# State-space stage of a two-block model: the loads, the convolution's filter taps and its gates in another order

## The reference, cut to what matters

```python
xbc = silu(dw_conv_centred(xbc, conv_w, conv_b))          # 5 taps along the tokens, per channel
xs, bm, cm = split(xbc)                                   # x per head, B and C per group
dt = softplus(dt + dt_bias)
# per direction, chunk by chunk, h carried on:
cum = cumsum(dt_c * -exp(a_log))
h_new = h * exp(cum[-1]) + einsum(b_c, exp(cum[-1:] - cum), x_c * dt_c)
seg = exp(where(lower, cum[i] - cum[j], -inf))
y = einsum(c_c . b_c, seg, x_c * dt_c) + einsum(c_c, h) * exp(cum)
# after both directions:
y = (y + d * x) * silu(z)
```

## Time and profile before

| | us |
|---|---|
| median of 3 runs | 5115.91 |
| lowest and highest | 5101.51, 5119.13 |
| the profiled execution | 5113.0 |
| its span | 5111.2 |
| start of the stage to the first step of group 0 | 72.70 |
| group 0, 1, 2, 3 | 96.90, 92.20, 92.20, 69.80 |

### The profile page before, as it was taken

One profiled execution on the slowest core, in us unless ns is written; L12 is line 12 of the kernel. 1 busy time (PEld: TensorE's weight loads), 2 busy tenths in 40 slices (PEclk: granted clock), 3 DMA queues, 4 the chain that ended last, 5 costly groups with the idle time before them and its releaser, 6 DMA issues. The chain is left out here.

```text
span 5111.2 us, 87975 instructions
## 1 busy us (share of the span) xinstructions
PE 4426.0 (87%) x38358; PEld 3445.9 (67%) x38358; DVE 2546.7 (50%) x3657; ACT 1593.3 (31%) x2530; POOL 502.2 (10%) x464
## 2 busy tenths in 40 slices
PE   7999969999897678786998777779999898887999
PEld 5888848877777456563332364568888786676787
DVE  4556667767775665542111315644442312675553
ACT  3222223333332453431000314432222212663332
POOL 0000021111110456000000003300000000000000
PEclk9999989999998789897999888889999999898999
DMA  6656720000001020426999520021122134112232
GB/s 244 228 201 217 268 76 23 15 15 14 14 6 38 19 70 17 170 79 250 421 421 422 212 95 18 24 103 58 62 67 71 66 115 143 38 62 87 83 103 91
DMA packets 165710, 604.18 MB, mean 118 GB/s; under 512 B 24192, under 2 KB 37376, under 8 KB 139984
## 3 DMA queue, kind: packets, MB, share of 16 engines
q1 hardware_dynamic: 152096, 538.78, 29.3%
q0 software_dynamic: 13232, 59.77, 3.0%
HBM read 527.03 MB, written 71.46 MB: 117 GB/s over the span
## 5 line engine op out<-in xcount | busy, mean ns | idle before, releaser
L2010 PE MATMUL f_acc<-f_a_lo,f_w_hi 128*128 128x512 f32 x4048 | 1034.9, 358 | 64.4 <-DVE f_a_lo L2232 30.5
L2010 PEld LDWEIGHTS f_acc<-f_a_lo,f_w_hi 128*128 128x128 f32 x4048 | 666.4, 190 | 187.2 <-issue 42.0
L2010 PE MATMUL f_acc<-f_a_lo,f_w_lo 128*128 128x512 f32 x2288 | 687.0, 356 | 0.0
L1999 DVE TENSOR_TENSOR f_w_lo<-f_w_raw,f_w_hi 128x1024 fp32r<-128x1024 f32 (+1 forms) x176 | 228.4, 1298 | 539.2 <-ACT f_w_hi L1994 539.2
L2010 PEld LDWEIGHTS f_acc<-f_a_lo,f_w_lo 128*128 128x128 f32 x2288 | 380.3, 190 | 67.7
L1994 ACT CAST f_w_hi<-f_w_raw 128x1024 fp32r<-128x1024 f32 (+1 forms) x176 | 194.8, 1107 | 611.0 <-DMA f_w_raw<-in_ffn_w_up 219.5
L2010 PE MATMUL i_acc<-i_x_hi,i_w_hi 128*128 128x512 f32 (+1 forms) x1024 | 306.6, 355 | 15.0 <-DVE i_x_lo L2787 10.0
L390 DVE COPY_PREDICATED rw_work<-rw_mask_x,rw_big 128x512 f32<-128x512 uint8 x288 | 238.4, 880 | 153.0 <-PE rw_big L690 147.9
L2010 PE MATMUL i_acc<-i_x_lo,i_w_hi 128*128 128x512 f32 (+1 forms) x1024 | 305.4, 354 | 0.0
L2010 PE MATMUL i_acc<-i_x_hi,i_w_lo 128*128 128x512 f32 (+1 forms) x1024 | 305.1, 353 | 0.0
L1417 PE MATMUL ex_big<-ex_w,ex_xe 128*64 128x512 f32 x1024 | 233.4, 611 | 31.8 <-DMA ex_w<-in_exp_w 31.1
(11 more groups left out here) (521 smaller groups left out, 8089.0 us busy)
## 6 DMA issues: line engine op xcount, KB each, us to landing
ex_w<-in_exp_w SPq DMA_DIRECT2D x192, 1024.0 KB, 16.3
i_mod_rows<-in_ada_rows SPq DMA_DIRECT2D x128, 512.0 KB, 4.7
f_w_raw<-in_ffn_w_up SPq DMA_DIRECT2D x88, 512.0 KB, 3.5
i_w_raw<-in_w_in_both SPq DMA_DIRECT2D x44, 512.0 KB, 3.6
f_w_raw<-in_ffn_w_down SPq DMA_DIRECT2D x32, 704.0 KB, 4.0
i_w_raw<-in_w_in_lat SPq DMA_DIRECT2D x40, 512.0 KB, 4.7
pt<-i_stage POOLq DMA_DIRECT2D x22, 768.0 KB, 5.9
f_w_raw<-in_hgrn_w_both SPq DMA_DIRECT2D x24, 512.0 KB, 3.5
```

Of the source, the lines that this page charges most:

```text
L1999: dve.tensor_tensor(self.view(self.w_lo, u), self.view(self.w_raw, u), self.view(self.w_hi, u).bitcast(F32), ALU.subtract).then_inc(self.r ...
L2010: op = pe.matmul(acc[:, a:b], part[:, k], xs[:, k0 + k, a:b], start=(first and k == 0 and part is w_hi and xs is x_hi), stop=(last and k = ...
```

## The change

It touches the start and the loop, on SP, DVE and ACT. PE's and POOL's instructions stand in the same order as before; PE's wait for the constants counts five transfers instead of seven.

- SP issues the step-size rows, their bias and the filter parameters (a semaphore `par_in` of their own), then group 0's rows, and behind these the five other constants.
- DVE clears only the three pads of each row of `raw` that no transfer or copy writes.
- At the start ACT permutes pair 0 ahead of the step-size chain, pairs 1 and 2 inside it; DVE takes taps of pairs 0, 1 and 2 between the chain's instructions and `silu` of pairs 0 and 1 ahead of the last product on `kinds`; ACT's gate of pair 2 stands behind `turned(0, 0..5)`.
- In the loop pair 1's taps stand at s = 4 (two), 5 and 6, pair 2's at s = 7 (two), 8 and 9; the gates of pairs 0 and 1 at s = 7 and their `silu` at s = 7 and 8; the gate of pair 2 at s = 10, its `silu` at s = 11.

```diff
+        TAPS = {4: ((1, 1), (1, 2)), 5: ((1, 3),), 6: ((1, 4),), 7: ((2, 1), (2, 2)), 8: ((2, 3),), 9: ((2, 4),)}
...
                 sp.dma_start(dtf[:, 0, :], pt[DT_T, 0:64, :]).then_inc(S["dt_in"], 16)
-                for dst, src in ((bias[:], dt_bias), (alog[:], a_log), (ident[:], consts["ident"]), (tri[:], consts["tri"]), (ones[:], consts["ones"]),
-                                 (skip[:], d_skip), (par[:].rearrange("p (g t) n -> p g t n", g=NG), params.rearrange("g p t n -> p g t n"))):
-                    sp.dma_start(dst, src).then_inc(S["const_in"], 16)
+                sp.dma_start(bias[:], dt_bias).then_inc(S["dt_in"], 16)
+                sp.dma_start(par[:].rearrange("p (g t) n -> p g t n", g=NG), params.rearrange("g p t n -> p g t n")).then_inc(S["par_in"], 16)
                 sp.wait_ge(S["pads"], 1)
                 load_group(0)
+                for dst, src in ((alog[:], a_log), (tri[:], consts["tri"]), (ident[:], consts["ident"]), (ones[:], consts["ones"]), (skip[:], d_skip)):
+                    sp.dma_start(dst, src).then_inc(S["const_in"], 16)
...
-                dve.memset(raw[:], 0.0)
+                dve.memset(raw[:, :, 0:2], 0.0)
+                dve.memset(raw[:, :, LAT + 2:LAT + 4], 0.0)
+                dve.memset(raw[:, :, CV_W - 2:CV_W], 0.0)
...
                 dve.drain().then_inc(S["dt_ready"], 1)
+                for k in range(1, CONV):
+                    conv_tap(0, 0, k)
+                dve.wait_ge(S["dt_abs"], 1)
...
+                conv_tap(0, 1, 1)
+                conv_tap(0, 1, 2)
+                dve.wait_ge(S["dtt_copied"], 1)
...
+                conv_tap(0, 1, 3)
+                conv_tap(0, 1, 4)
+                dve.wait_ge(S["const_in"], 80)
                 dve.tensor_copy(ident_r[:], ident[:])
...
                 dve.drain().then_inc(S["cums_done"], 1)
+                conv_tap(0, 2, 1)
+                conv_tap(0, 2, 2)
+                silu(0, 0)
+                silu(0, 1)
                 dve.wait_ge(S["kinds_done"], 1)
                 dve.tensor_tensor(flat(WJ), flat(WJ), flat(DT), ALU.mult)
                 dve.drain().then_inc(S["kinds_done"], 1)
-                for pair in range(3):
-                    for k in range(1, CONV):
-                        conv_tap(0, pair, k)
-                for pair in range(3):
-                    dve.drain()
-                    silu(0, pair)
+                conv_tap(0, 2, 3)
+                conv_tap(0, 2, 4)
+                dve.drain()
+                silu(0, 2)
...
-                            if 4 <= s < 8:
-                                conv_tap(g + 1, 1, s - 3)
-                            if s >= 8:
-                                conv_tap(g + 1, 2, s - 7)
-                            if s in (8, 9):
-                                silu(g + 1, s - 8)
-                    if more:
-                        dve.drain()
-                        silu(g + 1, 2)
+                            for pair, k in TAPS.get(s, ()):
+                                conv_tap(g + 1, pair, k)
+                            if s in (7, 8):
+                                silu(g + 1, s - 7)
+                            if s == 11:
+                                silu(g + 1, 2)
...
+                act.wait_ge(S["par_in"], 16)
+                permute(0, 0)
                 act.wait_ge(S["dt_ready"], 1)
...
+                act.wait_ge(S["const_in"], 80)
                 act.activation(alog[:], alog[:], ACT.Exp)
                 act.drain().then_inc(S["dt_abs"], 1)
+                permute(0, 1)
...
-                for pair in range(3):
-                    gate(0, pair)
-                for k in range(TURNS):
+                gate(0, 0)
+                gate(0, 1)
+                for k in range(6):
+                    turned(0, k)
+                gate(0, 2)
+                for k in range(6, TURNS):
                     turned(0, k)
...
-                        if more and s == 8:
+                        if more and s == 7:
                             gate(g + 1, 0)
                             gate(g + 1, 1)
+                        if more and s == 10:
+                            gate(g + 1, 2)
...
-                    if more:
-                        gate(g + 1, 2)
```

More of the change, by code:

```diff
@@ L847, in ssm @@
         TURNS = 9
-        names = ("const_in dt_in dt_ready dt_abs dtt_ready dtt_copied dta_ready cum_ready cums_done kinds_done masks_done pads group_in permuted tap_done conv_done "
+        TAPS = {4: ((1, 1), (1, 2)), 5: ((1, 3),), 6: ((1, 4),), 7: ((2, 1), (2, 2)), 8: ((2, 3),), 9: ((2, 4),)}
+        names = ("const_in dt_in par_in dt_ready dt_abs dtt_ready dtt_copied dta_ready cum_ready cums_done kinds_done masks_done pads group_in permuted tap_done conv_done "
                  "sig_done silu_done tr_ready tr_copied xw_done state_ready h_done inter_ready tmp_done row_ready exp_done g_done xdt_done xs_done skip_done "
@@ L923, in silu @@
                     dve.tensor_tensor(tiles(g, pair), tiles(g, pair), ex_tiles(pair), ALU.mult).then_inc(S["silu_done"], 1)
-                dve.memset(raw[:], 0.0)
+                dve.memset(raw[:, :, 0:2], 0.0)
+                dve.memset(raw[:, :, LAT + 2:LAT + 4], 0.0)
+                dve.memset(raw[:, :, CV_W - 2:CV_W], 0.0)
                 dve.memset(one[:], 1.0)
                 dve.drain().then_inc(S["pads"], 1)
-                dve.wait_ge(S["const_in"], 112)
-                dve.wait_ge(S["dt_in"], 16)
+                dve.wait_ge(S["dt_in"], 32)
                 dve.tensor_scalar(dtf[:, 1, 0:LAT].rearrange("p (c r) -> p c r", r=ROWS), dtf[:, 0, 0:LAT].rearrange("p (r c) -> p c r", c=GRID), bias[:, 0:1], None, ALU.add)
@@ L932, in _ @@
                 dve.drain().then_inc(S["dt_ready"], 1)
+                for k in range(1, CONV):
+                    conv_tap(0, 0, k)
+                dve.wait_ge(S["dt_abs"], 1)
+                dve.scalar_tensor_tensor(dtf[:, 0, :], dtf[:, 1, :], 0.0, dtf[:, 2, :], ALU.max, ALU.add)
+                dve.drain().then_inc(S["dtt_ready"], 1)
+                conv_tap(0, 1, 1)
+                conv_tap(0, 1, 2)
+                dve.wait_ge(S["dtt_copied"], 1)
+                for c in range(6):
+                    dve.scalar_tensor_tensor(kinds[:, DTA, c].rearrange("p d h -> p (d h)"), alog[:], -1.0, kinds[:, DT, c].rearrange("p d h -> p (d h)"), ALU.mult, ALU.mult)
+                dve.drain().then_inc(S["dta_ready"], 1)
+                conv_tap(0, 1, 3)
+                conv_tap(0, 1, 4)
+                dve.wait_ge(S["const_in"], 80)
                 dve.tensor_copy(ident_r[:], ident[:])
@@ L936, in _ @@
                 dve.drain().then_inc(S["masks_done"], 1)
[L937 to L943, removed]
                 dve.wait_ge(S["cum_ready"], 1)
@@ L1050, in _ @@
                 act.drain().then_inc(S["dtt_copied"], 1)
-                for pair in range(3):
-                    permute(0, pair)
+                permute(0, 2)
                 act.wait_ge(S["cum_ready"], 1)
@@ L1164, in cum_rows @@
                     last.then_inc(S["row_ready"], 1)
-                pe.wait_ge(S["const_in"], 112)
+                pe.wait_ge(S["const_in"], 80)
                 pe.wait_ge(S["dtt_ready"], 1)
```

## The result

The changed kernel takes 5129.7 us (median of 10 runs), the one before 5118.2 (10 runs): a ratio of 1.0031, 95% interval 1.0017 to 1.0044. The loss is real and small, some 11 to 20 us.

What follows compares the result with a forecast made beforehand. PE was taken to be held by waits: at the start, for exponentials behind a gate awaiting DVE's tap, and for pair 2's silu. 5.0 us a group, 15.0 for three, less 2.5: +12.5, 5128 us, range 5100 to 5145.

Steps and rivals of the forecast that it cites:

- start: Before group 0: rows and first turn come earlier, turn 6 waits for pair 2's gate; 2.5 us gained, bounds 0 to 5.9.
- (a): Loop step 4: two added DVE taps make PE wait for `tmp` in step 5; 0.6 us cost, bounds 0 to 1.4.
- (b): Loop step 7: PE's wait behind pair 1's gate moves up from step 8 and grows 2.9 us, to 6.0.
- (c): Loop step 10: pair 2's gate ahead of the exponentials, behind a late tap; 4.4 us cost, bounds 1.2 to 7.3.
- (d): Group's end: the gate and ACT's idle time go; 2.9 us gained, bounds 2.9 and 5.65.
- POOL's instructions alternate: Upper bound for step 4's added taps: POOL's instructions alternate with all of DVE's taps; 1.4 us cost.
- the waits vanish: Rival: loop taps run free and gates find columns done; 20.5 us less, 5095, lowest 5084; chance 0.08.
- Only an exchange: Rival: step 7's wait equals step 8's old one, pair 2's gate costs what the end returns; 5113 to 5122; chance 0.20.
- Slower by more: Rival: both loop waits leave PE slow for long; 29 us more, 5143; chance 0.20.
- The longer switch: Rival: each of six added table changes holds ACT another 1.28 us; 7.7 us more, 5136; chance 0.02.
- Table time: Theory of the experiments: gate and two table loads (1.28 + 1.49 + 1.28 us) cost that wherever they stand in the loop.
- Crowded DVE: Theory of the experiments: the doubled taps make `tmp` and the state late in the loop; the gates matter little.

Runs made afterwards that it cites:

- change_again: The changed kernel, unaltered, profiled and measured once more: 5136.6 us, ratio 1.0048 to the kernel before.
- start_only: The new start of the change with the loop of the kernel before: 5105.6 us.
- fewer_taps_at_4: The changed kernel without the two taps of step 4, which are left out of the convolution: 5116.1 us.
- gates_at_8: The changed kernel with the gates of pairs 0 and 1 back at s = 8, their silu at s = 8 and 9, taps still doubled: 5122.0 us.
- no_switch: The changed kernel with Exp in place of Sigmoid in the gates of groups 1 to 3, so no table loads beside them: 5124.9 us.
- no_last_tap: The changed kernel without the tap of step 9, left out of the convolution; gate and loads of step 10 stay: 5117.4 us.

## Why the prediction was right

It gave 5128 us (+12.5); measured are +11.5 and +19.6. That the first comparison comes within 2 us of the forecast is partly luck. The forecast added 5.0 us for a group, and the groups grew by 8.0 on average in the first profile and by 5.9 in change_again; in the first profile the rest of the program happened to be 8.0 us shorter than in the profile before (4749.2 against 4757.2). The second median, 5136.6, lies above the 5124 to 5134 to which the forecast was narrowed. The mechanism, though, is the one that was forecast: both waits, for late taps behind which the exponentials stand, and a small gain at the start and at the groups' ends. Its terms against the two profiles of the change, each as a difference from the same steps of before:

| | predicted | first profile, groups 0, 1, 2 | change_again |
|---|---|---|---|
| start | -2.5 | -2.8 | -2.9 |
| (a) + (b), steps 3 to 8 | +3.5 | +2.4, +3.8, +3.5 | +2.8, +2.7, +2.8 |
| (c), step 10 | +4.4 | +6.2, +6.2, +6.1 | +4.6, +4.6, +4.6 |
| (d), end | -2.9 | -1.9, -3.7, -1.7 | -3.0, -3.0, -3.0 |
| steps 0 to 2 | 0 | 0.0, +0.9, 0.0 | 0.0, +2.4, +2.4 |
| step 9 | 0 | 0.0, +2.2, 0.0 | 0.0, 0.0, 0.0 |

**The start** held step by step: rows at 1652.01 (1652.2 predicted), table load 1683.57 (1684.5), turn 0 at 1690.37 (1691.7), turn 6 at 1705.02 (1705.8), 0.2 to 1.3 us early, of which 0.55 is that this execution reached the stage sooner. start_only shows this gain by itself.

**(a)** 0.6 was the right kind and no fixed size: PE waits 0.95 us for `tmp` in step 5 in group 2 and nothing in two groups of change_again, but 3.12 in group 1 of the first profile, over twice the upper bound of 1.4. Four taps in a row took 7.11 in group 2 with POOL busy beside them, where the start before has sixteen in 16.16.

The bound "POOL's instructions alternate" has a rule for it in the Trainium skill ("SBUF — State Buffer", SBUF: two separate sides): DVE and GpSimd share a port pair, and where a DVE instruction has two inputs in SBUF and GpSimd's reads SBUF, the one that starts first holds the pair for its whole instruction and blocks the other. The rows agree in that a tap took 1.78 against 1.01; that each waited for whole instructions of the other, they do not show.

**(b)** was right in its cause in five of the six groups: the wait is moved a step up and lengthened by the taps put ahead. Its sum was right because two sizes were wrong in opposite directions. PE waits 4.3 to 4.6 and not 6.0, since pair 1's last tap ran nearly undisturbed (1.95 where 3.2 was reckoned); but the slow work behind the wait is 2.9 in group 2 (13.81 less 6.60 and 4.34) and up to 3.5 in change_again, and not 1.87. In group 1 of the first profile the +3.8 is a coincidence of sums: the wait for the gate was 1.44 there, and the rest is DVE's late `tmp`. fewer_taps_at_4 takes the lengthening away and leaves the wait; gates_at_8 takes the wait away; no_switch takes 1 to 2.5 us off the step of 13.8 to 14.6.

**(c)** stands too: PE got its product 12.1 us behind the state product of step 9, predicted 12.3 (1882.5 less 1870.2). That the slow work behind that wait would cancel against the waits that step 10 has anyway held in change_again and not in the first profile: after 4.05 and 4.04 us of waiting, the granted clock was 0.66 for the next 5.1 us in the one and 0.51 for 6.6 in the other. The lines of change_again:

```profile
1884.91 1.66 PE L1232 MATMUL ss_big<-ss_xdt,ss_seg 128*128 128x64 f32 x8 [4.05 <-POOL ss_seg L1144]
...
1884.91:1890.00 5.09, 5.09 (x30) 4.99 (x31) 0.00 (x0) 0.61 (x2) 2.27 (x2) 0.66 0.54 187
```

That goes with the difference of some 1.6 us a group, by which (c) was sized too small in the first profile. no_last_tap shows that all of (c) hangs on the late tap.

**(d)** came out at 3.0 in change_again. In the first profile groups 0 and 2 gave back less; PE was still at the low clock ahead of the end there (turn 6 took 1.91 in group 2 and 1.14 in group 1, which gave back 3.7).

**Not in the sum:** that ACT becomes the later one at a group's end was foreseen (PE stands 4.49 us for the copy of turn 6 in change_again), but not that PE comes out of this wait slow into the next group. In the windows of change_again, from this wait to that group's first steps, the granted clock stays low past the first state product at 1811.84:

```profile
1807.00:1812.00 5.00, 4.33 (x21) 4.06 (x20) 2.30 (x4) 3.83 (x5) 0.00 (x0) 0.50 0.01 3
1812.00:1816.00 4.00, 2.81 (x5) 0.47 (x3) 1.66 (x3) 3.92 (x5) 1.04 (x1) 0.81 0.58 198
1816.00:1820.00 4.00, 3.44 (x5) 1.59 (x6) 2.75 (x5) 3.92 (x6) 0.00 (x0) 0.62 1.00 324
```

In the profile of the kernel before, the granted clock was 1.00 from 1811 on, right behind the same product. Steps 0 to 2 of groups 1 and 2 are 2.4 us longer in change_again. That the slow clock makes all of the 2.4 was not tested.

Of the rivals, "the waits vanish" fell with the first state products of group 0. "Only an exchange" fell too: (a) + (b) cost 2.4 to 3.8 in every group, and (c) costs 1.6 to 4.4 more than (d) gives back. "Slower by more" describes the first profile in part (4.9 and 5.2 us of slow work behind both waits in groups 2 and 0), and the medians lie between it and the forecast. The longer switch fell with no_switch. Of the theories of the experiments, Table time fell with no_last_tap. Crowded DVE holds for (a), for 2.2 to 3.0 us of (b) and for what gates_at_8 kept in steps 8 and 9; in group 1 of the first profile it made most of the loss of steps 3 to 9.

## What to carry to other kernels

Work lent to another engine's queue must be ready when its turn in that queue comes: the distance between a column's last tap and its gate is worth more than the gate's own time. A gate two steps behind its last tap left 4 us of gate and table loads free (no_last_tap, step 10); a gate one step behind it cost 4.6 to 8 us (steps 10 and 7 of the change). So when work is pulled forward, pull all of its suppliers, or push its consumer back; here the order that wins spreads the taps and delays the gates.

## What the runs showed of the hardware

- After a wait of 4.34 us TensorE worked on at granted 0.50 (1.2 GHz) for 5.5 us although it had no further idle time; after waits of the same length (4.04 and 4.05 us) the two profiles of the change differ by some 1.6 us a step. Behind the waits of 4.0 to 4.6 us in steps 7 and 10 the step lost 0.5 to 3.5 us more than the wait itself.
- The ACT_TABLE_LOAD (1.28 us) ahead of a gate that waits lay inside that wait and cost nothing; the one behind it was paid, since no_switch, without both, took 1.42 us off PE's wait. In no_last_tap, where the gate waits for nothing, both were free.
- DVE's tap of 770 columns took 1.01 us alone (16 in 16.16) and 1.78 beside a busy GpSimd (4 in 7.11).
